# Laying the rows of a token group over the partitions in another order, in a gather and scatter of token rows beside a stream of expert weights

## The reference, cut to what matters

```python
def hier_moe(h, wg, bg, we, be, w_gate, w_up, w_down):      # N = 512 tokens, D = 2048
    g_prob = softmax(xt @ wg + bg)                          # 8 groups of 8 experts
    g_p, g_idx = lax.top_k(g_prob, 1)                       # one group for each token
    ...
    e_val, e_loc = lax.top_k(e_in, TOP_K_EXPERTS)           # two of the group's eight experts
    weight = g_p * softmax(e_val)
    ...
    def expert_chunk(args):                                 # w_*[e] are 2048 x 256 or 256 x 2048
        xc, e = args
        return (silu(xc @ w_gate[e]) * (xc @ w_up[e])) @ w_down[e]
```

## Time and profile before

| | |
|---|---|
| median of 3 runs | 1959.36 us (1957.67 to 1960.65) |
| the profiled execution, its own time | 1959.72 us |
| its span in the profile | 1957.9 us |
| TensorE matmul busy | 1871.3 us (96%) |
| TensorE weight load busy | 1354.0 us |
| VectorE, ScalarE, GpSimd busy | 706.1, 585.2, 245.4 us |
| moved by DMA | 505.92 MB |

### The profile page before, as it was taken

One profiled execution on the slowest core, in us unless ns is written; L12 is line 12 of the kernel. 1 busy time (PEld: TensorE's weight loads), 2 busy tenths in 40 slices (PEclk: granted clock), 3 DMA queues, 4 the chain that ended last, 5 costly groups with the idle time before them and its releaser, 6 DMA issues.

```text
span 1957.9 us, 28614 instructions
## 1 busy us (share of the span) xinstructions
PE 1871.3 (96%) x11946; PEld 1354.0 (69%) x11946; DVE 706.1 (36%) x1768; ACT 585.2 (30%) x1212; POOL 245.4 (13%) x208
## 2 busy tenths in 40 slices
PE   6999999999999999999999999989989899899996
PEld 5887777777777767788986666556566566655653
DVE  5331223333766668701142232313223123231322
ACT  5323333333544544322312232313113132131312
POOL 2433343333000000144100000000000000000000
PEclk9999999999999999999999999999999999999999
DMA  9554233233322331155589999999999999999994
GB/s 279 138 147 115 70 81 86 65 81 82 62 58 44 74 127 48 44 172 184 213 353 413 427 426 427 428 427 427 426 428 426 427 424 428 425 418 428 420 423 163
DMA packets 177394, 505.92 MB, mean 258 GB/s; under 512 B 52835, under 2 KB 136163, under 8 KB 151147
## 3 DMA queue, kind: packets, MB, share of 16 engines
q1 hardware_dynamic: 174954, 495.63, 66.2%
q0 software_dynamic: 2304, 8.39, 1.1%
HBM read 495.85 MB, written 16.53 MB: 262 GB/s over the span
## 4 chain that ended last, share of the span: by engine, by line
PE 79%; DMA 18%; ACT 1%; DVE 1%; issue 0%; SPq 0%; POOL 0%; POOLq 0%; ACTq 0%; DVEq 0%
PE banks L944 25%; PE banks L1352 12%; DMA at_region<-in_w_up 9%; PE banks L1101 9%; DMA x_region<-in_w_up 8%; PE banks L1377 7%; PE banks L1274 6%; PE banks L1353 3%; PE banks L1081 3%; PE banks L1053 2%; PE banks L1031 2%; PE banks L1323 2%; PE banks L993 1%; PE banks L1192 1%; PE banks L1038 1%; PE banks L1362 1%
## 5 line engine op out<-in xcount | busy, mean ns | idle before, releaser
L944 PE MATMUL banks<-ht_rounded,ring_rounded 128*128 128x512 f32 x1056 | 359.3, 394 | 0.7 <-ACT at_region L1515 0.7
L944 PEld LDWEIGHTS banks<-ht_rounded,ring_rounded 128*128 128x128 f32 x1056 | 195.1, 188 | 53.4 <-issue 13.8
L1352 PE MATMUL banks<-at_region,ht_region 128*64 128x256 f32 x800 | 180.7, 385 | 14.7 <-DMA at_region<-in_w_up 14.7
L848 POOL TENSOR_TENSOR ring_rounded<-ring_region,at_rounded 128x512 fp32r<-128x512 f32 (+1 forms) x92 | 115.9, 1291 | 511.1 <-ACT at_rounded L1454 511.1
L1353 PE MATMUL banks<-at_region,ht_region 128*64 128x256 f32 x768 | 175.4, 388 | 0.0
L2234 DVE SCALAR_TENSOR_TENSOR at_rounded<-banks,small,ring_rounded 128x512 fp32r<-128x512 f32 x128 | 96.1, 750 | 208.5 <-ACT ring_rounded L1740 207.6
L2227 DVE COPY consts<-banks 128x128 f32<-128x128 f32 x64 | 18.7, 292 | 403.7 <-PE banks L1362 403.7
L1352 PEld LDWEIGHTS banks<-at_region,ht_region 128*64 128x64 f32 x800 | 109.8, 139 | 72.7 <-issue 26.8
L1740 ACT ACTIVATE ring_rounded<-banks,small 128x512 fp32r<-128x512 f32 x128 | 88.0, 687 | 240.1 <-PE banks L1377 240.1
L944 PE MATMUL banks<-ht_rounded,at_rounded 128*128 128x512 f32 x352 | 142.7, 405 | 1.0 <-ACT at_region L1507 0.7
L1730 ACT ACTIVATE ring_region<-banks,consts 64x256 f32<-64x256 f32 x64 | 30.1, 470 | 374.6 <-PE banks L1353 374.4
(11 more groups left out here) (297 smaller groups left out, 3483.6 us busy)
## 6 DMA issues: line engine op xcount, KB each, us to landing
at_region<-in_w_gate SPq DMA_DIRECT2D x24, 2048.0 KB, 29.6
at_region<-in_w_up SPq DMA_DIRECT2D x23, 2048.0 KB, 28.8
at_region<-in_w_down SPq DMA_DIRECT2D x22, 2048.0 KB, 24.2
ring_region<-in_w_in SPq DMA_DIRECT2D x36, 1024.0 KB, 6.0
x_region<-in_w_down SPq DMA_DIRECT2D x17, 2048.0 KB, 26.9
x_region<-in_w_up SPq DMA_DIRECT2D x15, 2048.0 KB, 30.0
x_region<-in_w_gate SPq DMA_DIRECT2D x14, 2048.0 KB, 30.8
ring_region<-in_w_gate SPq DMA_DIRECT2D x9, 2048.0 KB, 34.2
```

Of the source, the lines that this page charges most:

```text
L848: ins = nc.gpsimd.tensor_tensor(w_low[n % RING][:, ks, 0:width], ring[n % RING][:, ks, 0:width], w_high[n % 2][:, ks, 0:width].bitcast(F32 ...
L944: ins = mm(out, w[:, k, 0:width], h[:, k, :], start=k == 0 and i == 0, stop=k == KT - 1 and i == 2)
L1352: mm(place[0:CAP, 0:D_EXPERT], x, gate[j], start=j == 0, stop=j == KT - 1)
```

## The change

The partition at which the r-th row of a group lies changes. Before, it is r. After, `row_iota` no longer holds the partition's own number but `rank`, the number of the row that lies there:

rank(p) = 2 * (p // 16) + (p // 4) % 2 + 16 * (p % 4 + 4 * ((p // 8) % 2))

So rows 0 to 15 lie at partitions 0, 4, 16, 20, 32, 36, ... 112, 116: two in each of the eight blocks of sixteen partitions. Rows 16 to 31 lie at 1, 5, 17, 21, ..., and so on. Every row number has one partition. `iota` (0 to 63), which the slots use, becomes a table of its own, so the table gets 64 columns more. `cap_rows` follows the same numbering. No instruction is added or taken away, and none changes its shape, but for the load of the table.

```diff
+CAP = 64
 C_IDENT = 0
...
 C_IOTA = C_DIAG + P
-C_TOK = C_IOTA + P
+C_RANK = C_IOTA + CAP
+C_TOK = C_RANK + P
...
-    c[:, C_IOTA:C_TOK] = np.arange(P)
+    rank = 2 * (p // 16) + p // 4 % 2 + 16 * (p % 4 + 4 * (p // 8 % 2))
+    c[:, C_IOTA:C_RANK] = np.arange(CAP)
+    c[:, C_RANK:C_TOK] = rank
...
-    c[:, C_ROWS:] = np.where(np.arange(P) < CAP, np.arange(P), -5000.0)
+    c[:, C_ROWS:] = np.where(rank < CAP, rank, -5000.0)
...
-        row_iota = consts[:, C_IOTA:C_IOTA + P]
+        row_iota = consts[:, C_RANK:C_RANK + P]
```

More of the change, by code:

```diff
@@ L215 @@
         SPLITS[step, 1].append((ALL_TILES + a, part))
-CAP = 64
 PASSES = T // CAP
```

## The result

The changed kernel takes 1962.62 us (median of 20 runs, 1960.28 to 1965.67), the kernel before 1959.55 us on the same chip (20 runs, 1957.51 to 1961.34). The ratio is 1.0016, with a 95% interval of 1.001 to 1.0022. That is 3.1 us slower. It is inside the 0.2% which the prediction took as the limit of what can be told, but with this many runs the interval excludes "no change". The forecast was 1945.5, and the range, 1941.5 to 1951.5, ended 11 us under the result.

The account below looks back on a forecast made before the run. The DMA weight stream was taken to set the pace from some 1220 to 1912 us. Gains of 12.0 us in the stream and 1.8 at scatter 7 made 13.8, so a median of 1945.5 us, range 1941.5 to 1951.5.

Parts of the forecast that it names:

- Which engine moves which row: Step on the gathers and scatters: two engines per sixteen partitions, told apart by the bit worth four; eight indices per engine.
- the term of 43 rows fewer: In 13 transfers within the weight stream the busiest engine's rows fall from 104 to 61: 13.2 us, taken as 12.0.
- The engines are dealt otherwise: Rival: engine given by partition bits 2 to 4 and 6, rows only 100 to 91, 1956.3 us; 4 in 100.
- a factor of 0.9: Scatters 1 to 6: excess over the weights 22.0 us of 24.6 due, so 13.2 us of gain was cut to 12.0.
- a small gain: Rival in the weight stream: the laggard had few rows and now gets 48 or so; 1950.3 us; 14 in 100.
- the cost is that of the busiest engine and not of the mean: Scatters 1 to 5: each group pays 4.9 us by the busiest engine, 2.8 by the mean; measured 5.1.
- 604.2 us from scatter 1 to 6: Sign: five groups with even rows ask for 122.2, 119.7, 121.6, 120.7 and 120.0 us or less.
- sum of 13.8 us: Whole gain forecast: 12.0 us in the weight stream plus 1.8 us at scatter 7.
- The table's cost of nothing: Load at the start: 32 KB more of table costs 0 to 0.1 us, counted at nothing.
- Scatter 7 was to give 1.8 us: Last scatter, at the end of everything: eight rounds of rows become two, 1.8 us off the end.
- TensorE's waits were to fall to 33 us: Sign in the expert stage: TensorE's 45 us of waits for up matrices shrink to 33 or so.
- the signs named for an error: Wrong if TensorE's busy time per group grew, scatter 7 still took eight rounds, or groups stayed at 123 us with even rows.

Follow-up runs that it names:

- e1: The changed kernel's longer table, but row r back at partition r as in the kernel before; 1959.4 us against 1959.31 for the kernel before.
- e2: The changed kernel with the order of before, the two halves of the partitions swapped; 1965.55 us against 1959.31 for the kernel before.
- e4: The changed kernel with partition bit 3 turned round, putting rows on the eight engines it left nearly empty; 1963.08 us against 1959.31 for the kernel before.
- e7: The changed kernel with sixteen successive rows on the eight even-numbered engines; 1962.98 us against 1959.43 for the kernel before.
- e9: The changed kernel with the row counts of before, the largest dealt to engines 5, 6 and 9 to 14; 1965.74 us against 1959.19 for the kernel before.
- e10: The changed kernel with the row counts of before, the largest dealt to engines 0 to 4, 7, 8 and 15; 1959.34 us against 1959.19 before.
- e5: e3 with the engines of partitions 64 to 127 first in each sixteen rows; 1954.98 us against 1959.43 for the kernel before.
- e8: The changed kernel with rows dealt by weight, 0.6 for engines 5, 6 and 9 to 14, 1 for the others; 1951.93 us against 1959.19 before.
- e3: The changed kernel with sixteen successive rows over all sixteen values of partition bits 2, 3, 4 and 6; 1951.9 us, again 1951.36, against 1959.31 and 1959.43 before.
- e6: The changed kernel with rows dealt by weight, 1 for engines 0 to 7 and 0.65 for 8 to 15; 1953.99 us against 1959.43 before.
- e11: e10 with its two largest counts on engines 3 and 7, and 76 rows on engines 0 and 1; 1961.79 us against 1959.88 for the kernel before.

## Why the prediction was wrong

**The step that failed is "Which engine moves which row".** It read the starts of scatter 7 as three engines and eight rounds, and took two engines for each block of sixteen partitions, told apart by the bit worth four. In truth partitions 0 to 18 lie on five engines, with 4, 4, 4, 4 and 3 rows. Two errors made the other reading fit. The stretch in which five packets are at work was passed over: the prediction counted 4 rows in it and still wrote that never more than three engines work. And two of the five engines start their rows late: in e1, with the same rows on the same engines, the 0.3 us stretches from the first row on have 4, 4, 4, 3, 2, 2 and 2 large packets (two of them of q14), which five engines give when two of them begin late. A count of what starts at one time is no count of engines. The 54 rows of gather 0, which seemed to confirm the rule, lie on eight engines by either rule, and so could not tell them apart. The rule with bits 2 to 4 and 6, which the prediction had named and set aside because of this reading, is the one that the runs follow. With it, sixteen successive rows of the changed order lie on eight engines, two on each, and the term of 43 rows fewer becomes 100 - 91 = 9 rows, 2.8 us and not 12.0.

**The rival that had the engines right had the sign wrong.** "The engines are dealt otherwise", put at 4 in 100, gave 91 rows and 1956.3. Measured was 6.3 us more. What it lacks, e2, e4, e7 and above all e9 against e10 show: some engines carry another load beside the rows. The candidate is the instruction queue q8. Between 1100 and 1900 us, before as after:

```profile
q8 instruction: 42, 0.69, 0.3%
q14 instruction: 9, 0.07, 0.0%
```

These are 42 packets of q8, 16 KB each. What follows is read from the landing records, which no row above shows: a weight load signals 16 times, once for each engine, and the records have the times of all sixteen, though not which engine each is of. After each packet of q8 one engine is about 1.5 us later than it was against the others. Followed one engine at a time, the packets go round eight engines in turn; which eight is an inference from the runs in which one or the other set of engines had the rows: 5, 6 and 9 to 14. The records bear it out in e9 and e10: in the steps of 1.5 us that stand clear of the transfers, the engine set back is always one of the ten earliest of the sixteen in e10, whose rows are off these eight, and always one of the seven latest in e9, whose rows are on them. That is 42 / 8 = 5.25 packets for each of them, some 8.0 us or 26 rows' worth at 0.307 us.

The expectations from e5 on reckon with six or seven of these packets on each engine and with a lead of 1.9 us that engines 0 to 7 have at the start of the stream; e8 and e10 do not bear out that lead, so what follows takes the 42 packets and no lead. The rule then is: the pace is that of the engine with the most rows, counting 26 more for each of the eight. Before that is 78 + 26 = 104 on engine 5, just over engine 0 with 100. What it asks of each run, against what was measured:

| run | the most loaded engine | asked, us | measured, us |
|---|---|---|---|
| the change | 89 + 26 = 115 | +3.4 | +3.1 |
| e2 | 100 + 26 = 126 | +6.8 | +6.2 |
| e3, and again | 55 + 26 = 81 | -7.1 | -7.4, -8.1 |
| e4 | 90 + 26 = 116 | +3.7 | +3.8 |
| e5 | 61 + 26 = 87 | -5.2 | -4.4 |
| e6 | 62 + 26 = 88 | -4.9 | -5.4 |
| e7 | 88 + 26 = 114 | +3.1 | +3.6 |
| e8 | 73 | -9.5 | -7.3 |
| e9 | 100 + 26 = 126 | +6.8 | +6.5 |
| e10 | 100 | -1.2 | +0.1 |
| e11 | 100 | -1.2 | +1.9 |

Asked is the difference to 104, times 0.307, and stands for the stream alone; measured is the difference of the medians. The table was made after the runs. It would explain why nine rows fewer cost 3.1 us: the change moved rows from engines without these packets to engines 5, 9, 12 and 13, which have them.

The profiled executions give the stream by itself, from the load that lands at 1122.4 us before to the up matrix at 1912.6 and the same two in each run: the change +2.3 us, e2 +4.7, e3 -7.5 and -7.3, e4 +3.3, e5 -6.4, e6 -5.1, e7 +2.2, e8 -7.6, e9 +7.0, e10 -0.6, e11 +1.9. Against the medians it is right within 1 us in the eight orders where one of the eight is the last. In the three where another one should be the last it asks for 1.3 to 3.1 us too little, some 4 to 10 rows' worth.

The landing records say where most of it is: in the other instruction queue, q14, whose nine packets of 8 KB the count leaves out. In e11 three of them (at 1250, 1452 and 1819 us) set the last engine back by 0.9 to 1.0 us each, 2.9 together; in e10 the same three fall on an engine that is not the last, and two others (at 1198 and 1614 us) set the last one back by some 0.65 us each. With these added, the rule asks for +1.7 in e11 (measured +1.9) and +0.1 in e10 (measured +0.1), and in e8 two of them fall on the last engine as well. In the kernel before it puts engine 0 or 1, with 100 rows and 1.3 us, level with the 104 of engine 5, so the other lines stay as they are. This was read after the runs, and no run was made for it.

The Trainium skill (DMA: Bandwidth & Descriptors, Latency and other measured facts) has engines 7 and 15 as usually slower where GpSimd issues the transfers; it would fit e11, which has 100 rows on engine 7 where e10 has 78, but no run here tells whether it is engine 7 or engine 3, which has 100 rows there as well.

So it is shown that where the rows lie decides, by which bits the engine is given, and that the same rows on other engines differ by some 6 us in this stream. That the difference is the instruction packets is argued from the landing records and their agreement with the eleven orders, not shown by a run: no kernel with fewer instruction packets was tried. Nor can these runs part an engine from the partitions that it serves.

**The group before scatter 6.** The prediction took a factor of 0.9 from it and wrote that "the engine that was last is not the one with the rows". It was a warning, but half of it has a plainer cause. Between scatters 5 and 6 lie scatter 5 and gather 7, whose 19 rows put 4 on the busiest engine and not 8. So 12 rows were due there, 3.7 us, against the 1.5 that the scatters show, and from scatter 1 to 6 not 24.6 us but 23.3, of which 22.0 were paid. The rest can be the packets, which make now one engine the last and now another: in the records of the kernel before, a step of 1.5 us brings another engine to the end at 1578 us and again at 1730. In the changed kernel this group took 122.52 us. This is the rival "a small gain" turned round, an engine with a load of its own that got more rows; that rival was given 1950.3 because its engine was taken to have had few rows before and to get 48.

**What held.** The stream bounds the kernel, and the cost is that of the busiest engine and not of the mean: e3, whose sixteen engines are even, is 11 us faster than the change with the same number of rows. The size of that term was right where the layout did what the prediction thought: it asked for 604.2 us from scatter 1 to 6 (122.2 + 119.7 + 121.6 + 120.7 + 120.0), and e3 again took 604.35. The close match is in part luck: e3 the first time took 605.92, and the five groups of e3 again are 121.54, 121.66, 120.01, 122.32 and 118.82. But its sum of 13.8 us would not have come about with the even layout either: e3 gave 7.4 and 8.1, by the rule above because the most loaded engine falls from 104 to 81 rows' worth, 23 and not 43. The table's cost of nothing holds (e1). Scatter 7 was to give 1.8 us and gave 1.5, but not by the rounds named: its rounds go from four to three, 0.3 us; the rest goes with engines that no longer start late, and is not settled, since e3, with two rounds, is no shorter (3.4 us from issue to landing, after 3.1, before 4.6), and e2, with four rounds as before, ends 4.2 us after the start of its scatter 7 where the kernel before takes 5.5. TensorE's waits were to fall to 33 us and fell to 41.9. One of the signs named for an error came in part: the groups stayed at 122 to 124 us, though not with even rows. Scatter 7 did not take eight rounds, in either kernel.

## What to carry to other kernels

Before rows are dealt over DMA engines, find out which partition is served by which engine with a count that must come out differently under each rule, for instance how many large packets are under way at once in a lone transfer, over all its stretches of 0.3 us: the first stretch alone shows three rows here where five engines serve. Where a stream fills all engines, the time is that of the engine with the most work of every queue, so count the small queues in microseconds for each engine and not as a share of sixteen; by the account above, a share of 0.3% was worth more here than the nine rows. The best order of these runs is e3, one row on each of the sixteen engines in turn, 0.9962 and 0.996 of the time before, and weights on top of it (e8) gave nothing more.

## What the runs showed of the hardware

- An indirect DMA with one index for each partition is dealt over the engines by partition bits 2, 3, 4 and 6: 19 rows at partitions 0 to 18 use five engines, and 19 rows over all sixteen values have 15 rows under way in one 0.3 us stretch at 437 GB/s.
- The engines run far apart in a full stream. By the landing records, the 16 parts of one weight load land within 2.0 us of each other at 1147 us and within 17.2 us at 1907 us in the kernel before, and within 11.0 us at 1909 us in e3 again. All slices show nine tenths or more in both, so a full slice does not show that the load is even.
- The same counts of rows on other engines changed the time by 6.4 us (e9 against e10). By the landing records, an instruction packet of 16 KB sets one engine back by about 1.5 us; the packet's own record takes 1.06 us (mean of the 42), and at the 27.3 GB/s of the rows it would be 0.6. One of 8 KB of q14 sets one back by 0.6 to 1.0 us.
